# Expert rows and results in high and low fp32r parts, with gates at the evacuation and weights packed by the host

## The reference

```
def swiglu(h, w1, w3, w2):
    return (jax.nn.silu(h @ w1) * (h @ w3)) @ w2

def moe_swiglu(h, w_router, w1, w3, w2):
    logits = (h @ w_router).astype(jnp.float32)
    top_v, top_i = lax.top_k(logits, TOP_K)
    gates = jax.nn.softmax(top_v, axis=-1)
    combine = jnp.sum(jax.nn.one_hot(top_i, N_EXPERTS, dtype=jnp.float32) * gates[..., None], axis=-2)
    out = jnp.zeros_like(h)
    for e in range(N_EXPERTS):
        out = out + combine[..., e:e + 1].astype(h.dtype) * swiglu(h, w1[e], w3[e], w2[e])
    return out
```

## Time and profile before

| | |
|---|---|
| Runs | 1758.38, 1761.59, 1762.69 us (median 1761.59) |
| Profiled execution, its own time | 1761.89 us |
| Its span, first to last instruction | 1760.0 us |
| Mean granted TensorE clock | 0.974 |
| Busy: TensorE matmul / VectorE / ScalarE / GpSimd | 1648.2 / 1336.6 / 1059.4 / 112.1 us |
| Chain that ended last, by engine | PE 74%, DVE 11%, ACT 5%, issue 5%, DMA 4% |
| Loads of expert weights | 336 of 1 MB, median 8.3 us from issue to landing |

### The profile page before, as it was taken

One profiled execution on the slowest core, in us unless ns is written; L12 is line 12 of the kernel. 1 busy time (PEld: TensorE's weight loads), 2 busy tenths in 40 slices (PEclk: granted clock), 3 DMA queues, 4 the chain that ended last, 5 costly groups with the idle time before them and its releaser, 6 DMA issues.

```text
span 1760.0 us, 27088 instructions
## 1 busy us (share of the span) xinstructions
PE 1648.2 (94%) x9618; PEld 1418.2 (81%) x9618; DVE 1336.6 (76%) x1250; ACT 1059.4 (60%) x1039; POOL 112.1 (6%) x151
## 2 busy tenths in 40 slices
PE   6888969999797897799999999999999999999997
PEld 5877859999797786688888888888888888888886
DVE  4888555444458865788888888888888888888885
ACT  4634454433353335477677677677777777676775
POOL 1142100000005210000000000000000000000000
PEclk8999989999899999799999999999999999999999
DMA  7520036452352103499999999999999999999993
GB/s 230 159 72 25 16 120 216 165 192 95 119 168 71 42 1 118 143 356 363 311 366 351 321 368 358 323 366 356 325 366 338 340 367 327 352 366 328 347 367 114
DMA packets 327137, 427.99 MB, mean 243 GB/s; under 512 B 6849, under 2 KB 294753, under 8 KB 326961
## 3 DMA queue, kind: packets, MB, share of 16 engines
q1 hardware_dynamic: 326304, 425.28, 71.8%
q0 software_dynamic: 640, 2.00, 0.4%
q10 hardware_dynamic: 144, 0.05, 0.0%
HBM read 426.25 MB, written 1.05 MB: 243 GB/s over the span
## 4 chain that ended last, share of the span: by engine, by line
PE 74%; DVE 11%; ACT 5%; issue 5%; DMA 4%; SPq 0%; DVEq 0%; ACTq 0%; POOL 0%; POOLq 0%
PE bank L375 29%; PE bank L400 15%; PE bank L1121 8%; PE bank L378 7%; PE bank L628 6%; PE bank L403 4%; DMA ring<-in_moe_w 3%; ACT wh L435 2%; DVE wl L439 2%; PE bank L660 1%; PE bank L388 1%; PE bank L1126 1%; DVE ml L615 1%; DVE hs L1877 1%; DVE rw L1779 1%
## 5 line engine op out<-in xcount | busy, mean ns | idle before, releaser
L439 DVE TENSOR_TENSOR wl<-ring,wh 128x2048 fp32r<-128x2048 f32 x369 | 844.6, 2293 | 211.4 <-ACT wh L435 198.8
L435 ACT ACTIVATE wh<-ring 128x2048 fp32r<-128x2048 f32 x369 | 705.9, 1915 | 130.2 <-PE bank L400 43.5
L375 PE MATMUL bank<-wh,xh 128*128 128x512 f32 x896 | 361.7, 404 | 0.9 <-DVE xl L868 0.9
L375 PE MATMUL bank<-wh,xl 128*128 128x512 f32 x896 | 351.1, 392 | 0.0
L375 PE MATMUL bank<-wl,xh 128*128 128x512 f32 x896 | 349.6, 390 | 0.0
L375 PEld LDWEIGHTS bank<-wh,xh 128*128 128x128 f32 x896 | 168.4, 188 | 37.5 <-issue 4.9
L375 PEld LDWEIGHTS bank<-wh,xl 128*128 128x128 f32 x896 | 168.3, 188 | 37.3
L375 PEld LDWEIGHTS bank<-wl,xh 128*128 128x128 f32 x896 | 169.0, 189 | 32.0
L400 PE MATMUL bank<-wh,gh 128*128 128x512 f32 x448 | 175.5, 392 | 3.5 <-DVE gl L525 3.4
L400 PE MATMUL bank<-wh,gl 128*128 128x512 f32 x448 | 174.6, 390 | 0.0
L400 PE MATMUL bank<-wl,gh 128*128 128x512 f32 x448 | 174.6, 390 | 0.0
(11 more groups left out here) (294 smaller groups left out, 2564.3 us busy)
## 6 DMA issues: line engine op xcount, KB each, us to landing
ring<-in_moe_w SPq DMA_DIRECT2D x336, 1024.0 KB, 8.3
ring<-in_ffn_w SPq DMA_DIRECT2D x33, 1024.0 KB, 6.1
ring<-in_w_in SPq DMA_DIRECT2D x24, 1024.0 KB, 5.3
ring<-in_w_out SPq DMA_DIRECT2D x8, 1024.0 KB, 5.1
ring<-in_w_in SPq DMA_DIRECT2D x2, 640.0 KB, 4.0
const<-in_const SPq DMA_DIRECT2D x1, 1200.0 KB, 14.4
proj<-in_x SPq DMA_DIRECT2D x4, 256.0 KB, 6.7
out<-wide SPq DMA_DIRECT2D x1, 1024.0 KB, 4.0
```

What stands on the lines that cost most here:

```text
L375: ins = nc.tensor.matmul(up_bank(run, par, 0)[:], x[:, 0:C], w[b][:, k], **kw)
L435: nc.scalar.activation(o, src[0], ACT.Copy).then_inc(sem("w_high"), 1)
L439: nc.vector.tensor_tensor(split(wl[:, buf]), src[0], split(wh[:, buf]).bitcast(F32), ALU.subtract).then_inc(sem("w_split"), 1)
```

## The change

- **Gather.** ScalarE rounds the transposed rows of h to hh (fp32r) straight from the banks, VectorE subtracts to hl. sel is fp32r (it holds 0 and 1). Each product of the gather becomes two fp32r matmuls, hh and hl by sel. They are of 128 columns.
- **Gates.** GpSimd also builds place, the 0/1 matrix of slots. TensorE transposes place, not selg, and adds two fp32 matmuls of selg by a matrix of ones with 8 columns: the gate of each slot. ScalarE copies that to gslot and the transpose to placed (fp32r).
- **Result.** ScalarE evacuates the accumulator with the gate as scale, rounded to yh; VectorE makes yl (a new scalar_tensor_tensor per bank) from the same bank, gslot and yh. The scatter is two fp32r matmuls, yh and yl by placed.
- **Accumulator.** zero_acc is gone; the first matmul of a bank in the first down projection has start=True. For that pe_steps takes its first step out of the loop.
- **Weights.** The host lays each tile out as 128 rows of 8 KB (for w_in's last unit 5 KB), so that each load is one contiguous block.

```diff
@@
-        def pe_down(pe, run, m, last=False):
+        def pe_down(pe, run, m, last=False, first=False):
...
                             ins = nc.tensor.matmul(bank[2 + o][:], g[:, a, 0:C], w[b][:, a, o * 512:(o + 1) * 512],
-                                                   start=False, stop=False, skip_group_check=True)
+                                                   start=first and a == 0 and g is gh and b == 0, stop=False, skip_group_check=True)
@@
-            with pe.Fori(0, n // 2) as i:
-                step(2 * i + 1, 1)
+            step(1, 1, True)
+            with pe.Fori(0, (n - 1) // 2) as i:
                 step(2 * i + 2, 0)
-            if n % 2:
-                step(n, 1)
+                step(2 * i + 3, 1)
+            if (n - 1) % 2:
+                step(n, 0)
@@
             def gather(j):
...
-                            mm(bank[5 + half][:, d * C:(d + 1) * C], hrows()[:, tt, k * P:(k + 1) * P], sel[:, tt],
-                               tt == 0, tt == 1, "gathered" if d == 3 and tt else None)
+                            mm(bank[5 + half][:, d * C:(d + 1) * C], hh[:, tt, k * P:(k + 1) * P], sel[:, tt], tt == 0, False)
+                            mm(bank[5 + half][:, d * C:(d + 1) * C], hl[:, tt, k * P:(k + 1) * P], sel[:, tt], False, tt == 1,
+                               "gathered" if d == 3 and tt else None)
 
             def turn_gates(j):
                 pe.wait_ge(sem("selg_built"), j + 1)
                 for tt in range(TT):
-                    turn(bank[7][:, tt * P:(tt + 1) * P], selg[:, tt], sig="gates_turned" if tt else None)
+                    turn(bank[7][:, tt * P:(tt + 1) * P], place[:, tt])
+                for tt in range(TT):
+                    mm(bank[7][:, T:T + NE], selg[:, tt], cst("ones")[:, 0:NE], tt == 0, tt == 1, "gates_turned" if tt else None)
 
             def scatter(j):
 
                 pe.wait_ge(sem("gates_copied"), j + 1)
-                pe.wait_ge(sem("acc_copied"), 2 * j + 2)
+                pe.wait_ge(sem("y_low"), 2 * j + 2)
...
-                        mm(bank[SCATTER[b]][:, k * T:(k + 1) * T], yj[:, dt * P:(dt + 1) * P], pgt[:],
-                           sig="scattered" if k else None)
+                        mm(bank[SCATTER[b]][:, k * T:(k + 1) * T], yh[:, dt * P:(dt + 1) * P], placed[:], True, False)
+                        mm(bank[SCATTER[b]][:, k * T:(k + 1) * T], yl[:, dt * P:(dt + 1) * P], placed[:], False, True,
+                           "scattered" if k else None)
...
                 pe.wait_ge(sem("scatter_added"), 4 * (j - 1) + 2)
-                zero_acc((2, 3))
                 pe_steps(pe, nxt)
@@ ScalarE
-                copy(hrows()[:, :, b * T:(b + 1) * T], bank[b][:].rearrange("p (a t) -> p a t", a=TT), "h_copied")
+                nc.scalar.activation(hh[:, :, b * T:(b + 1) * T], bank[b][:].rearrange("p (a t) -> p a t", a=TT), ACT.Copy
+                                     ).then_inc(sem("h_high"), 1)
...
-                nc.scalar.copy(pgt[:], bank[7][:, 0:T]).then_inc(sem("gates_copied"), 1)
+                nc.scalar.copy(gslot[:], bank[7][:, T:T + 1]).then_inc(sem("gslot_ready"), 1)
+                nc.scalar.activation(placed[:], bank[7][:, 0:T], ACT.Copy).then_inc(sem("gates_copied"), 1)
...
-                    nc.scalar.copy(yj[:, half * 512:(half + 1) * 512], bank[2 + half][:]).then_inc(sem("acc_copied"), 1)
+                    nc.scalar.activation(yh[:, half * 512:(half + 1) * 512], bank[2 + half][:], ACT.Copy, scale=gslot[:, 0:1]
+                                         ).then_inc(sem("y_acc_high"), 1)
@@ VectorE, before the copy of pos (L846)
+            for b in range(4):
+                dve.wait_ge(sem("h_high"), b + 1)
+                hv = slice(b * T, (b + 1) * T)
+                nc.vector.tensor_tensor(hl[:, :, hv], bank[b][:].rearrange("p (a t) -> p a t", a=TT), hh[:, :, hv].bitcast(F32),
+                                        ALU.subtract).then_inc(sem("h_low"), 1)
@@ VectorE, in the loop after up(0, 0, 0, 1)
+            def acc_low(j):
+                dve.wait_ge(sem("gslot_ready"), j + 1)
+                for half in range(2):
+                    dve.wait_ge(sem("y_acc_high"), 2 * j + half + 1)
+                    hv = slice(half * 512, (half + 1) * 512)
+                    nc.vector.scalar_tensor_tensor(yl[:, hv], bank[2 + half][:], gslot[:, 0:1], yh[:, hv].bitcast(F32),
+                                                   ALU.mult, ALU.subtract).then_inc(sem("y_low"), 1)
...
                 up(0, 0, 0, 1)
+                acc_low(j - 1)
                 up(1, 0, 1, 0)
@@ GpSimd
+                nc.gpsimd.tensor_tensor(place[:], hit[:, 0], hit[:, 1], ALU.add).then_inc(sem("gates_chain"), 1)
@@ SyncE
-                        load(slot, slot_of(slot), w[bass.ds(row13, D), bass.ds(m * T, T)].rearrange("(k p) n -> p k n", p=P))
+                        load(slot, flat_slot(slot), w[bass.ds(row + m * P, P), :])
```

More of the change, by code:

```diff
@@ L242, in program @@
         gate = sb("gate", [P, 2, T])
-        yj = sb("yj", [P, D])
-        sel = sb("sel", [P, TT, C])
+        yh = sb("yh", [P, D], F32R)
+        yl = sb("yl", [P, D], F32R)
+        hh = sb("hh", [P, TT, D], F32R)
+        hl = sb("hl", [P, TT, D], F32R)
+        sel = sb("sel", [P, TT, C], F32R)
+        place = sb("place", [P, TT, C])
+        gslot = sb("gslot", [P, 1])
         selg = sb("selg", [P, TT, C])
@@ L248, in program @@
         hit = sb("hit", [P, 2, TT, C])
-        pgt = sb("pgt", [P, T])
+        placed = sb("placed", [P, T], F32R)
         rt = sb("rt", [P, T])
@@ L404, in pe_down @@
                                                    w[b][:, a, o * P:(o + 1) * P], g[:, a],
-                                                   start=False, stop=False, skip_group_check=True)
+                                                   start=first and o % 2 == a == b == 0 and g is gh, stop=False, skip_group_check=True)
                 if last and not run.moe and o % 2 and o < KT - 1:
@@ L410, in pe_steps, with step @@
         def pe_steps(pe, run):
-            def step(m, par):
+            def step(m, par, first=False):
                 pe_up(pe, run, m, par, 0)
@@ L950, in load, with sp_ffn @@
                 sp.dma_start(dst, src).then_inc(sem(f"w_ready{slot}"), 16)
-            def columns(slot, w, at, n):
-                load(slot, ring[:, slot, :, 0:n], w[:, at:at + n].rearrange("(k p) n -> p k n", p=P))
             def mixer_unit(layer, u):
-                if u < NU:
-                    columns(u % RING_M, A["w_in"][layer], UNITS[u][0], UNITS[u][1])
-                else:
[L959 to L965, removed]
+                slot = u % RING_M
+                if u < NU - 1:
+                    load(slot, flat_slot(slot), A["w_in"][layer, u])
+                elif u == NU - 1:
+                    load(slot, flat_slot(slot)[:, 0:KT * UNITS[u][1]], A["w_in_end"][layer])
+                else:
+                    load(slot, flat_slot(slot), A["w_out"][layer, u - NU])
+            def sp_ffn(run, w1, w3, w2, row, after_mixer):
                 def free(slot, first, n):
@@ L2080, in parameters, with column_tiles, row_tiles, up_tiles @@
     return np.ascontiguousarray(np.concatenate(rows).T)
+def column_tiles(w, at, n):
+    w = np.asarray(w)[..., at:at + n]
+    w = w.reshape(*w.shape[:-2], KT, P, n)
+    return np.ascontiguousarray(np.swapaxes(w, -3, -2)).reshape(*w.shape[:-3], P, KT * n)
+def row_tiles(w):
+    w = np.asarray(w)
+    w = w.reshape(-1, 2, P, D)
+    return np.ascontiguousarray(np.swapaxes(w, 1, 2)).reshape(-1, 2 * D)
+def up_tiles(w):
+    w = np.asarray(w)
+    w = w.reshape(w.shape[-3], KT, P, w.shape[-1] // T, T)
+    return np.ascontiguousarray(w.transpose(0, 3, 2, 1, 4)).reshape(-1, KT * T)
+def weights(inputs):
+    w_in = inputs["w_in"]
+    full = [column_tiles(w_in, at, n) for at, n, _ in UNITS[:-1]]
+    out = {"w_in": np.stack(full, 1), "w_in_end": column_tiles(w_in, *UNITS[-1][:2]),
+           "w_out": np.stack([column_tiles(inputs["w_out"], o * T, T) for o in range(NO)], 1)}
+    for n in ("ffn_w1", "ffn_w3", "moe_w1", "moe_w3"):
+        out[n] = up_tiles(np.asarray(inputs[n]).reshape(-1, D, inputs[n].shape[-1]))
+    for n in ("ffn_w2", "moe_w2"):
+        out[n] = row_tiles(inputs[n])
+    return {n: np.ascontiguousarray(a) for n, a in out.items()}
 def kernel(**inputs):
@@ L2088 @@
     arrays = {f"in_{n}": np.ascontiguousarray(inputs[n]) for n in NAMES}
+    arrays.update((f"in_{n}", a) for n, a in weights(inputs).items())
     arrays["in_const"] = constants()
```

44 lines of the change are left out of this document (20 added, 24 removed).

## The result

The changed kernel takes 1764.38 us in the median of 17 runs (1762.75 to 1765.83), the one before 1760.18 us beside it (17 runs). The ratio is 1.0021 with a 95% interval of 1.0014 to 1.0029: a real loss of some 3.7 us (4.2 between the medians) that stays within the 0.3% that the forecast called no change. The forecast was 1761.6 us, a difference of +0.05 us, with a range of 1750 to 1771. The profiled execution took 1765.2 us, its span is 1763.3 us (before 1760.0).

A forecast was written before the change was run, and what follows sets the result against it. TensorE, VectorE and DMA stood close together in the expert stage, with the change acting at job boundaries; −4.25 − 3.7 + 1.9 + 3.3 + 1.6 + 1.2 = +0.05 us gave 1761.6 us against the median, range 1750 to 1771.

The forecast's parts named there:

- Packed weights, −4.25: Expert stage loads: longer rows bring a step's DMA to 7.8 us, under TensorE's 8.43, removing late-load excess at boundaries: −4.25 us.
- Rival four: Weight loads: longer rows don't raise the DMA rate, so the 4.25 us stay and time is 1766 us; chance 0.10.
- Zeroing dropped, −3.7: Job boundaries: zeroing stands after TensorE's wait for the adds, so its 0.53 us counts in full, seven times: −3.7 us.
- Gather, +1.9: Gather at boundaries: 32 single-pass matmuls at 0.120 us each, paced by the weight load, +0.27 us seven times: +1.9 us.
- The rival at 0.227: Gather: narrow single-pass matmuls are no faster than fp32, 0.227 us each, 7.3 us for 3.57; time 1789 us; chance 0.16.
- the one at 0.067: Gather: weight load is shorter than 8-column rows say; gather takes 2.1 us, −1.7 per boundary; time 1750 us; chance 0.10.
- Gates, +3.3: Ahead of the last down projection: two added fp32 matmuls of 8 columns cost 0.48 us, seven times: +3.3 us.
- Accumulator, +1.6: Boundary chain on ScalarE: each accumulator copy with a scale operand takes 0.11 us longer, +0.23 per boundary, seven times: +1.6 us.
- Rival two: Boundaries: VectorE has no room for yl, costing up to 9 us, time 1770 us; chance 0.12.
- Scatter, worth nothing: Scatter at boundaries: 1.9 us for 3.6, but the adds wait for VectorE, so TensorE only idles longer; worth nothing.
- Start, +1.2: the step that failed: Start of the experts: four hl on VectorE, 2.5 us against 1.44 us idle, delay the first gather: +1.2 us (0 to +2.8).
- End, 0 (±0.5): Kernel end: yl delays the last scatter 0.7 us, shorter matmuls and the squares behind the adds offset it: 0 (±0.5) us.

## Why the prediction was right, and where it wasn't

The total was right within the forecast's own bounds, in part by luck: two errors of opposite sign stand in it, 1.7 us in the jobs and 4.4 at the start and the end. The difference, forecast as nothing, came out as a small loss clear of the noise.

- **Packed weights, −4.25.** Right: −4.5 in the jobs, −4.1 in the median. The place was right too: ScalarE waited 15.0 us for loads before and 1.6 after. That the wait before the split would go held for five of the seven boundaries. Rival four is dead (a share of 0.95 at 375 GB/s).
- **Zeroing dropped, −3.7.** Too large: −2.7. I counted the zeroing's whole 0.53 us because it stands behind the wait, but the up matmul in its place starts 0.16 us later.
- **Gather, +1.9.** Mis-sized: 0.112 us for each instruction, not 0.120, and so as long as the fp32 one. From the transposes ahead of it to those of the gates it is 3.75 us for 3.79, which makes −0.3 over seven. The sizes fit the mechanism: 8 columns go at 0.119 in the earlier trace rows, 128 at 0.112, 256 at 0.117, 512 at 0.227, so below 256 columns something else than the columns sets the pace. That it is the weight load is argued and not shown, since no run changes the weights alone. The rival at 0.227 and the one at 0.067 are both dead. The 81 ns of the Trainium skill, "TensorE: Matmul & The Clock Gate", section "Back-to-back issue gap", aren't reached with these fp32r operands: 0.112 in all seven boundaries. Its section "LDWEIGHTS (loading the stationary operand)" puts a load, in ns, at its columns over 1.2, which for 128 columns is an estimate of 107 ns. The 0.112 us between starts come near to that; the loads' own rows in both traces overlap and are longer, 0.19 us each.
- **Gates, +3.3.** Right. From the start of the transposes to the down projection it is 0.61 us after and 0.13 to 0.14 without them, 0.47 × 7 = 3.3.
- **Accumulator, +1.6.** Nearly: from the start of yh to the next split it is 1.16 us, and 0.96 for yj, and the adds come 0.18 later after the scatter's start: 7 × 0.18 = +1.3.
- **yl, 0.** Right in the loop, with 0.49 us left of the idle time. Rival two would have needed that gone.
- **Scatter, worth nothing.** Right for the loop, and shown by undoing it: 886.51 against 886.58 us. Idle 2.08 us, forecast 1.9. What it left out is that such an idle time can let the clock fall (two of seven in one run).
- **Start, +1.2: the step that failed.** It came to +4.5. The hl part was about +1.0. The other 3.5 is the clock: I had priced the first gather at 0 beyond hl, taking it that the clock comes back as in the kernel before, 4.4 us after the gather starts. With the fp32r gather it came back only 13.7 us after. From the gather's start to the first up matmul it is 8.47 us (before 7.34), and from there to job 0's first transposes 10.71 (before 8.29): +1.1 and +2.4. Undoing the gather took all 4.5 back, hl's 1.0 with them; filling TensorE's wait ahead of it took 3.6 back. The filled wait shows that the loss is the clock's. What keeps the clock low is less sure, since undoing the gather also shortens the idle time ahead of it (4.36 us for 5.33). For the gather itself speaks that TensorE then worked without a gap for 6.6 us at 1.2 GHz and the clock didn't rise, where it rose after 4.4 us of the fp32 gather; and that it came the same way in all nine profiles that leave the wait unfilled: the clock was low for 17.07 us in the three with fp32r, for 6.83 in the six with fp32.
- **End, 0 (±0.5).** It came to +1.1, again by the clock. yl stands in the last chain, where there is nothing to hide it:

```profile
1742.96 1.41 DVE L900 SCALAR_TENSOR_TENSOR yl<-bank,gslot,yh 128x512 fp32r<-128x512 f32 x2 [3.83 <-ACT yh L800]
1744.43 0.39 PE L1143 MATMUL bank<-placed,yh 128*128 128x256 f32 x1 [2.22 <-DVE yl L900]
...
1746.95 4.72 PE L1143 MATMUL bank<-wide,const 128*128 128x256 f32 x16
```

The scatter waits 2.22 us, where before it waited 1.16 for yj. I had set the shorter matmuls against that. But the clock falls at 1745.76, during this scatter, and the sixteen matmuls of the last norm take 4.72 us, for 3.62 before. The same 3.41 us, from 7.97 us behind job 7's last transposes on, in the kernel after and in the one with the filled wait, which has the same code here:

```profile
1745.76:1749.17 3.41, 3.41 (x13) 2.96 (x13) 2.02 (x4) 2.89 (x5) 0.00 (x0) 0.50 0.00 0
```

```profile
1740.47:1743.88 3.41, 3.29 (x18) 2.73 (x18) 1.92 (x4) 2.90 (x5) 0.00 (x0) 1.00 0.00 0
```

With the clock up in this stretch the end takes 24.69 us, and 24.64 in the kernel with the fp32 gather. So yl and the short scatter together cost 0.2 us, inside the forecast's ±0.5, and the early fall of the clock some 0.9. It came in three of the five profiles with the 2.22 us wait and in none of the five without.

By stretches: jobs −4.5 (packing) − 2.7 (zeroing) − 0.3 (gather) + 3.3 (gates) + 1.3 (accumulator) = −2.9 (measured −2.8), against −1.15 forecast; start and end +5.6, against +1.2. The rest of the 3.3 us between the spans is the 0.5 of spread ahead of the router. The first boundary's 0.6 us that I took as a mean was 0.84 (20.22 − 19.38), part of the reason that packing gave 4.5.

Open: why the clock stays low for longer at the fp32r gather. The runs show that it does and that filling the wait before it helps, not what in the gather's activity decides it; a run with the fp32 gather behind the full 5.33 us of idle time would part the gather from the idle time, and there is none. Also open is when an idle time of 2.1 us lets the clock fall and when not.

## What to carry to other kernels

Price a faster instruction at what stands behind it: the halved scatter bought only a wait for VectorE, and the best version kept both small products in fp32 and instead repacked the weights, dropped the zeroing and moved one wait to where its banks are first written (ratio 0.9941, where the whole change has 1.0021). When matmuls get thinner, read the granted clock row of the stretch behind them, and of every idle time that they leave. Extra instructions that the loop hides in another engine's idle time come out at its two ends: the four hl cost 1.0 us there, the two yl, with the shorter scatter behind them, 0.2, and the clock near them more than both.

## What the runs showed of the hardware that was not expected

- A run of 32 single-pass fp32r matmuls of 128 columns, each with its own weights, behind 5.33 us of idle time, was part of 17.07 us at 1.2 GHz in three profiles; 32 instructions of an fp32 gather, behind 4.35 or 4.36 us of idle time, of 6.83 us in six.
- An idle time of TensorE of 1.96 to 2.11 us was followed by 3.41 us at 1.2 GHz in three cases (one at the start with filled wait, two with the fp32 gather), and by nothing in the other five boundaries of that second kernel, in the seven of the first and in the seven of the kernel after.
- 128 x 128 fp32r matmuls with their own weights go at 0.112 us, 256 columns at 0.117 in the scatter: half of the columns save 4%. In the fp32 gather the distance is 0.112 as well, two instructions for each product.
- Counted from the start of the adds that TensorE waits for, an up matmul starts 0.16 us later (1.50 us) than a small zeroing matmul in its place (1.34).
